# Four raw and five split weight buffers instead of six and four, with splits issued four tiles ahead instead of three

## What is computed

```
mod = silu(c) @ ada_w + ada_b                       # 2048 x 12288, for c and c_ctx
z   = modulate(rmsnorm(x), sh1, sc1) @ w_in         # q, k, v of attention; r, k, v, w, a, g of RWKV
zc  = modulate(rmsnorm(xc), sh1c, sc1c) @ w_in      # the same for 256 context tokens
attn = windowed_gqa(q, k, v, kc, vc, sink)
rw   = RWKV scan, forward and backward, over context and x
x = x + g1 * (concat(attn, rw) @ w_out)
x = x + g2 * ((silu(h @ w1) * (h @ w3)) @ w2)
x = rmsnorm(x)
mem_n = rmsnorm(mem);  mk, mv = mem_n @ w_mem_kv    # for two layers
x = x + concat(retention(x), memory attention) @ w_out_a
kv = rmsnorm(x) @ w_kv
x = x + concat(dilated attention(x, kv), memory attention) @ w_out_b
out = rmsnorm(x)
```

## Time and profile before

| | |
|---|---|
| median of 3 runs | 3760.32 us (3759.24 to 3764.66) |
| profiled execution, its own time | 3766.6 us |
| its span, first to last instruction | 3764.6 us |
| granted TensorE clock, mean | 0.986 of full speed |
| TensorE matmul busy | 3633.8 us (97%) |
| VectorE busy | 2289.3 us (61%) |
| ScalarE busy | 1691.1 us (45%) |
| DMA, mean rate | 178 GB/s |

### The profile page before, as it was taken

How to read it: one execution, slowest core, us unless ns; L and a number is a source line. 1 busy time by engine, 2 the same in 40 slices (tenths; PEclk the granted TensorE clock), 3 DMA queues, 4 the chain that set the end, 5 groups by cost and what they waited for, 6 DMA issues and landing times.

```text
span 3764.6 us, 67168 instructions
## 1 busy us (share of the span) xinstructions
PE 3633.8 (97%) x27944; PEld 3152.6 (84%) x27944; DVE 2289.3 (61%) x3020; ACT 1691.1 (45%) x2219; POOL 153.3 (4%) x187
## 2 busy tenths in 40 slices
PE   8999999899998999999999999999999999999998
PEld 5778888778777888888888888977888888888897
DVE  3467777767656676555566666556555555555555
ACT  3442236655444444444454445444444444444443
POOL 0000000011110000000000011000000000000000
PEclk9999999999999999999999999999999999999999
DMA  9876774000034676566555555455655555555554
GB/s 338 313 249 234 294 276 150 17 3 3 22 130 164 228 261 219 192 190 189 186 174 176 176 171 181 150 173 162 208 170 183 174 173 172 175 174 176 171 165 143
DMA packets 183501, 668.76 MB, mean 178 GB/s; under 512 B 20480, under 2 KB 20608, under 8 KB 182560
## 3 DMA queue, kind: packets, MB, share of 16 engines
q1 hardware_dynamic: 177408, 645.12, 51.4%
q10 hardware_dynamic: 4512, 15.14, 1.2%
q0 software_dynamic: 1280, 4.20, 0.3%
HBM read 655.98 MB, written 8.39 MB: 176 GB/s over the span
## 4 chain that ended last, share of the span: by engine, by line
PE 83%; DVE 8%; ACT 4%; issue 3%; DMA 3%; POOL 0%; DVEq 0%; SPq 0%; ACTq 0%; POOLq 0%
PE ps L1156 69%; DVE whl L2234 2%; ACT whl L1672 2%; PE ps L1394 1%; PE ps L1407 1%; DMA raw<-in_mem 1%; PE ps L1660 1%; PE ps L1644 1%; DVE tm L2237 1%; PE ps L1299 1%; PE ps L1103 1%; ACT work L1672 1%; PE ps L1386 1%; DVE x L2237 1%; PE ps L1460 0%
## 5 line engine op out<-in xcount | busy, mean ns | idle before, releaser
L1156 PE MATMUL ps<-halves,whl 128*128 128x256 f32 (+1 forms) x14752 | 2571.0, 335 | 44.9 <-DVE whl L2234 14.4
L1156 PEld LDWEIGHTS ps<-halves,whl 128*128 128x128 f32 x14752 | 2237.7, 190 | 348.1 <-issue 47.3
L2234 DVE TENSOR_TENSOR whl<-raw,whl 128x1024 fp32r<-128x1024 f32 x1016 | 1243.2, 1238 | 847.3 <-ACT whl L1672 846.1
L1672 ACT ACTIVATE whl<-raw 128x1024 fp32r<-128x1024 f32 x1016 | 1053.9, 1053 | 893.2 <-PE ps L1156 639.0
L1156 PE MATMUL ps<-whl,halves 128*128 128x256 f32 x2752 | 486.3, 335 | 2.6 <-DVE whl L2234 2.6
L1156 PEld LDWEIGHTS ps<-whl,halves 128*128 128x128 f32 x2752 | 417.8, 189 | 62.0 <-issue 8.5
L1672 ACT ACTIVATE work<-ps 128x512 f32<-128x512 f32 (+1 forms) x202 | 115.2, 574 | 313.0 <-PE ps L1156 268.5
L2234 DVE TENSOR_TENSOR work<-work,ps 128x512 f32<-128x512 f32 x155 | 106.2, 685 | 126.4 <-ACT work L1672 126.4
L2337 DVE SCALAR_TENSOR_TENSOR raw<-raw,mix 128x1024 f32<-128x1024 f32 x128 | 153.3, 1222 | 0.0
L1672 ACT ACTIVATE xw<-xw,cols 128x384 f32<-128x384 f32 (+1 forms) x32 | 24.9, 778 | 147.3 <-DVE cols L2240 147.3
L1672 ACT ACTIVATE Xt<-ps 128x512 f32<-128x512 f32 x96 | 57.2, 598 | 51.3 <-PE ps L1407 49.9
(11 more groups left out here) (277 smaller groups left out, 2286.2 us busy)
## 6 DMA issues: line engine op xcount, KB each, us to landing
raw<-in_ffn SPq DMA_DIRECT2D x264, 512.0 KB, 4.1
raw<-in_w_kv SPq DMA_DIRECT2D x192, 512.0 KB, 3.6
raw<-in_w_in_b SPq DMA_DIRECT2D x160, 512.0 KB, 3.5
raw<-in_adaT SPq DMA_DIRECT2D x128, 512.0 KB, 5.5
raw<-in_w_in_a SPq DMA_DIRECT2D x128, 512.0 KB, 3.7
raw<-in_ada SPq DMA_DIRECT2D x64, 512.0 KB, 5.6
raw<-in_mem SPq DMA_DIRECT2D x64, 512.0 KB, 6.0
raw<-in_w_out_a SPq DMA_DIRECT2D x48, 512.0 KB, 4.2
```

The costliest lines, as they stand in the source:

```text
L1156: p = self.e.matmul(o, x, y, start=bi not in begun, stop=final and kc == 3 and m == len(pairs) - 1, skip_group_check=True)
L1672: return self.e.activation(out, in_, func, **kw)
L2234: return self.e.tensor_tensor(out, a, b, op)
```

## The change

The raw ring shrinks from six buffers to four and the split ring grows from four pairs to five, in the same space (6 + 2 x 4 = 4 + 2 x 5 = 14 buffers of 4 KB a partition). Splits are written one tile further ahead. The RWKV buffers that share the space get new places in it, with the waits that go with them.

```diff
--- before.py
+++ after.py
@@ -15,9 +15,9 @@
-NRAW = 6
-NW = 4
-AHEAD = 3
+NRAW = 4
+NW = 5
+AHEAD = 4
@@ -131,11 +131,10 @@
-EARLY_LOADS = {GATE + i: (at, free) for i, (at, free) in enumerate((
-    (2, ("pre_mm", (7, "v"))), (3, ("pre_v", (7, "bh"))), (4, ("inv_mm", (7, 5, 1, "Xt"))), (5, ("inv_mm", (7, 5, 1, "T1"))),
-    (0, ("adv_mm", (7, "U"))), (1, ("adv_mm", (5, "Z")))))}
-EARLY_SPLITS = {GATE + i: free for i, free in enumerate((
-    ("inv_mm", (7, 5, 1, "x")), ("adv_mm", (7, "U")), ("adv_mm", (7, "Y")), ("adv_mm", (7, "Y"))))}
+RAW_FREE = ((0, ("pre_mm", (7, "v"))), (1, ("pre_v", (7, "bh"))), (2, ("inv_mm", (7, 5, 1, "Xt"))), (3, ("inv_mm", (7, 5, 1, "T1"))))
+SPLIT_FREE = (("inv_mm", (7, 5, 1, "x")), ("adv_mm", (7, "U")), ("adv_mm", (7, "U")), ("adv_mm", (7, "Y")), ("adv_mm", (7, "Y")))
+EARLY_LOADS = {GATE + i: (at, free) for i, (at, free) in enumerate(RAW_FREE)}
+EARLY_SPLITS = {GATE + i: free for i, free in enumerate(SPLIT_FREE)}
@@ -1960,7 +1959,8 @@
-            self.wait_ge("mm", TILES[GATE - 5].n)
+            self.wait_ge("hi", TILES[GATE - 3].n)
+            self.wait_ge("lo_v", TILES[GATE - 3].n)
@@ -2526,7 +2526,8 @@
-            self.wait_ge("mm", TILES[GATE - 6].n)
+            self.wait_ge("hi", TILES[GATE - 4].n)
+            self.wait_ge("lo_v", TILES[GATE - 4].n)
@@ -3062,7 +3063,7 @@
-AR_AT = (128 * 256, 32 * 256)
+AR_AT = (128 * 256, 44 * 256)
@@ -3084,7 +3085,7 @@
-    at("whl", 24 * K, [2, NW, 1024], F32R)
+    at("whl", 4 * NRAW * K, [2, NW, 1024], F32R)
@@ -3121,7 +3122,7 @@
-    for i, n in enumerate(("Xt1", "btok1", "lw", "Pinv", "X1", "BT1", "ktok1", "AKA1", None, "vtok1", "wup", "w0r", "U", "Z")):
+    for i, n in enumerate(("lw", "Pinv", "X1", "BT1", "AKA1", "Xt1", "U", "vtok1", "ktok1", "w0r", "btok1", None, "Z", "wup")):
```

## The result

| | before | changed |
|---|---|---|
| median, first group of runs | 3759.78 us (4 runs, 3756.04 to 3764.66) | 3809.19 us (4 runs, 3794.69 to 3810.51) |
| median, second group of runs | 3760.47 us (8 runs) | 3798.74 us (4 runs, 3796.06 to 3810.52) |
| profiled execution | 3766.6 us | 3794.69 us |
| its span, mean granted clock | 3764.6 us, 0.986 | 3792.6 us, 0.985 |

The change is slower: ratio 1.0123 (95% interval 1.0109 to 1.0136) in the first group, 1.0109 (1.0092 to 1.0125) in the second. The runs of the changed kernel scatter over 16 us, those of before beside them over 9 and 5 us; over all its 38 runs in this study, before covers 14 us (3750.86 to 3764.96).

What follows compares the result with a forecast made beforehand. TensorE, busy 97% of the span, bounds the kernel, so only its waits cost. Terms 15 + 5 + 4 + 5 + 3 + 3 - 8 = 27 us, added to 3760.3, gave 3787 us; range 3764 to 3820.

Steps and rivals of the forecast that it cites:

- The mem/ada stage: 35 to 205 us: `mem` loads issued one pair later, so a pair takes 4.03 us against 3.71; 15 us lost (1 to 33).
- Pairs: mem/ada stage: the slower pace of tile pairs, 0.32 us for each of 48 pairs, 15 us lost.
- other loads: mem/ada stage: loads for context, x and c in the same queue take the place of tiles; 5 us lost (0 to 11).
- The start: Kernel start: four `ada` tiles load early instead of six, two more loads wait behind the gate; 4 us lost (2 to 6).
- w_k to w_va: 300 to 500 us: VectorE frees the buffers, two rounds of load and step per block; 5 us lost (0 to 14).
- w_q: 500 to 560 us: loading already sets the pace, less one tile of extra lead; 3 us lost (0 to 6).
- ffn2 with adaT: To 1423 us: rounds of load and step make 14 us where TensorE needs 11.1; 3 us lost (0 to 7).
- The gain: Mostly after 1260 us: one more split tile repays waits that a split ends; 8 us gained (3 to 14).
- The RWKV ends: Ends of the RWKV stage: renamed space and changed waits cost nothing; 0, within 2 us either way.
- Everything heavy: Rival, whole kernel: landing time stays at 6.1 us and VectorE's stage becomes load-bound; 3833 us, from 3800 on; chance 0.22.
- The tie: Rival, whole kernel: landing time falls to about 4.5 us and the gain repays most; 3755 to 3767 us; chance 0.13.
- the faster case: Rival, whole kernel: landing time of 4.1 us makes the gate free, split lead repays waits; 3752 us; chance 0.10.

Runs made afterwards that it cites:

- change_mem_first: The changed kernel, with SyncE issuing each `mem` load of the mem/ada stage ahead of the `ada` load before it: 3781.44 us, ratio 1.0057 to before.
- raw4_only: The kernel before with four raw buffers instead of six, still four split pairs and splits three tiles ahead: 3805.95 us, ratio 1.0117.
- lead3_only: The changed kernel's rings (four raw buffers, five pairs), with splits written three tiles ahead as before instead of four: 3801.15 us, ratio 1.0112 to before.
- raw5_only: The kernel before with five raw buffers instead of six, split ring and written order as before: 3773.36 us, ratio 1.0035.
- before_mem_first: The kernel before, with each `mem` load issued ahead of the `ada` load that stands before it: 3753.46 us, ratio 0.9985.

## Why the prediction was right, and where it was not

The prediction was right in sign and in its main mechanism, and 3809 us lies in its range. Its 27 us are met by the profiled executions (28.1 us apart), and are too few for the medians: the eight executions of the change have a median of 3804.7, 45 us over before. That the sum meets the profile is in part luck, for errors cancel in it: a wait of 5 us at 226 us was not in it and `ffn2` cost 3.5 us more, while `w_k` to `w_va` cost nearly 5 less and the other terms some 3 less. Point by point:

- **The mem/ada stage: right as to the gate, with one term missing.** Landing time 4.8 us for the 5.0 I took, pair 4.02 us for 4.03; change_mem_first shows that the gate on the `ada` step is the cause. The waits are fewer and longer than I said: 13 in all, 1.1 us each on the mean, not 0.2 to 0.5 before every `mem` tile. Pairs (15) and other loads (5) made 20 us. Between 30 and 224 us the two traces of the change lose 20.1 and 19.6, four others with the same gate 24.6 to 25.4; the pace of pairs explains (4.02 - 3.71) x 48 = 15. So 5 us for the other loads held in the change, and 10 was nearer in the others. What makes the +25.1 of the change is the turn at 226 us: 5.0 us, of which the gate has some 1.4 (raw4_only) and splits written four ahead the rest. I had said that AHEAD does not help here; that it can hurt I had left out. The lower clock was also left out of the sum (I had said so under the rivals): 0.85 from 35 to 75 us, against 0.92, is 2.8 us.
- **The start: right,** 3.2 to 5.4 us for 4. The gated loads take 15.09 us, two more of them, where they took 9.83:

```profile
17.92 15.09 SPq L3039 DMA_DIRECT2D raw<-in_ada  x12
34.71 0.33 SPq L3039 DMA_DIRECT2D raw<-in_mem  x1
```

- **w_k to w_va: the 5 us were not there.** No trace loses more than 0.4 us up to 450 us; what is lost just before 500 us, up to 3.6 us more, lies at the held-up evictions told under lead3_only. The step that failed is the choice between my two ends. VectorE's idle time did swallow the rounds of load and step: waits of VectorE, 330 to 530 us of the change,

```profile
DVE whl L2234 <- ACT whl L1671: 32.5, 27, 2.1
DVE xk L2237 <- ACT xk L1671: 3.8, 1, 3.8
```

  where it had stood idle 14.2 us ahead of four evictions `xk` before, and 5.3 us for splits. It now arrives at the evictions just in time. The loads helped: the `adaT` tiles land in 4.6 us (DMA issues, 330 to 530 us), not the 5.8 of the earlier trace rows.

```profile
raw<-in_adaT SPq DMA_DIRECT2D x72, 512.0 KB, 4.6
```

- **w_q: right,** 2.0 to 3.8 us for 3, if what is lost just before 500 us is left to the stage before; from 450 to 560 us it is 2.4 and 6.2. I had taken off a tile of lead for it, and the three-ahead kernels lose 4.6 and 4.9. **ffn2 with adaT: too small,** 6.5 us for 3, near its upper end of 7. TensorE came short in seven waits of up to 1.2 us; I had let leads absorb more than they did.
- **The gain: near in size by the traces, wrong in place.** Over raw4_only the change gains 5.1 us between 650 and 1390 us, 1.1 in `ffn2` and 3 behind, 9 in all; I had 8. The medians cannot confirm it: they differ by 7.2 us in the group where both ran, but the change's first group lies above raw4_only. The wait I had counted on first, 4.98 us, gave nothing: another wait took its place, and with the clock it became a loss of 2.3. The 2.06 us at 1129 us went, 3.5 us with what followed, but 3.2 of them went in raw5_only too. And 2.5 us came near 1218 us, from a wait for `halves` and not for a split, of a kind that I had said is not shortened. No run has the fifth pair with nothing else changed.
- **The RWKV ends:** no loss shows that belongs to them.
- **The size.** The terms of the change's own trace sum to what I had, by the cancelling told above. What is missing to the medians seems to be in two things. I took the profiled execution of before, 6.3 us over its median, as if the changed kernel would keep that distance; instead the change was profiled in one of its fastest executions. All eleven other traces are faster than before's between 650 and 1390 us, even raw4_only (2.9 us) and before_mem_first (0.9), which have nothing that would help there; this points to 1 to 3 us of bad luck in the reference. And the stages up to 515 us scatter upwards, by up to 8 us at 226 us and 12 at 515, which a sum from one median latency can't show. How much of the 17 us each of the two holds stays open.
- **The rivals.** Everything heavy (3833) fell, since the landing time dropped with the pace, as I had argued. The tie and the faster case fell with the gate: L was 4.8, above the 4.5 and 4.1 that they need. As an estimate by the Trainium skill (SBUF — State Buffer, "The DMA setup-cost knee") the second tile of a pair would land in 4.0 us. The runs have 4.8 in the gated stage and 6.1 before, so the measurement decides against it here as a figure for a loaded stage; the `mem` loads of raw5_only, first of their pair, landed in 3.8 from 150 to 205 us and in 4.5 from 60 to 205.

## What to carry to other kernels

A ring is worth what its most tightly coupled stage makes of it: count how many products lie between the event that frees a buffer and the use of what is loaded into it, and compare with the landing time, before taking a buffer away. When a queue issues in order, the order of issue can be worth as much as the buffers: putting the load with the long way (load, split, product) ahead of the one that is used raw recovered 17 of the change's 38 to 49 us without any memory, and made the old kernel faster too. Writing work further ahead in a queue is not free either: a split that stands ahead of an eviction and waits for its load holds the eviction up, 3.6 us at one place here. And look behind a wait before paying to remove it: if the engine's next need comes from a chain that does not move, the wait moves instead.

## What was not expected of the hardware

- Landing time fell with the number of buffers at the same rate. With two buffers fewer, `mem` loads went from 6.1 to 4.8 us and `adaT` loads from 5.8 to 4.6, the latter at nearly the same rate in the `w_k` stage (286 GB/s before, 284 in the change). change_mem_first has it for the `mem` loads too: 4.8 us at 314 GB/s from 60 to 205 us, where before has 6.1 at 313. The last two buffers of six thus seem to have held transfers that mostly queued there.
- A lower granted clock goes with the waits and adds to what they cost: 0.84 for 14 us after one wait of 4.42 us, 0.85 against 0.92 from 35 to 75 us, and 1.00 instead of 0.93 where a wait of 4.1 us went down to 1.3. Which part each wait has in it was not tried.
- A stage without slack seems to spread: the same program was 27.0 to 34.5 us late at 226 us in four executions.
